# A layer's expert units on VectorE: two loops and one fixed buffer order

## The chip, the cores and the metric

The kernel runs on one core of one Trainium2 chip. The metric is device time in microseconds; the time before is the median of three runs.

## The reference

A trunk of two pre-norm residual layers over 256 tokens of width 2048. Layer 0 mixes tokens with a bidirectional mLSTM, layer 1 with grouped-query attention. After each mixer comes the same channel mixer, PEER, which is what the change touches:

```python
def peer(xn, wq, k1, k2, u, v):
    q = (xn @ wq).reshape(B, S, 8, 2, 128)
    s1, s2 = ...                      # scores of 8 heads against 128 + 128 keys
    t1, i1 = lax.top_k(s1, 16)
    t2, i2 = lax.top_k(s2, 16)
    cand_s = all 256 sums t1[a] + t2[b];  cand_i = i1[a] * 128 + i2[b]
    top_s, pos = lax.top_k(cand_s, 16)
    idx = cand_i at pos;  gate = softmax(top_s)
    # for each token and each of its 8 * 16 experts e, weight gate[e]:
    act = gelu(dot(x, u[idx]))
    y = sum over e of gate[e] * act[e] * v[idx]
```

Each token picks 16 experts per head out of 16384, and each expert is a row of u and a row of v, 2048 floats each.

## The kernel before

The work of a PEER layer is cut into 16 units: two blocks of 128 tokens by 8 heads. A unit has 16 tiles. A tile is one expert for each of the 128 tokens of the block: 128 rows of u and v together, 16 KB a row, 2 MB in all. So there are 256 tiles in a layer and 512 in the kernel.

Every tile goes the same way:

- POOL (`gathers`, the DMA at L551) waits on `v_used` until PE has used up the buffer and issues an indirect DMA from the table of experts into it. There are six buffers (`NUV = 6`, `uv_slot`), which lie in `ring_sb`. Tile t of a layer goes into buffer t mod 6 (`slot_of`), so a buffer's last tile is always the sixth before. POOL issues the gathers in order; once a unit it copies the 16 indices first (L539).
- VectorE (`expert`, L1683) waits for the landing of that buffer and takes the dot product of the u rows with the tokens, 128 x 2048. After each odd tile it handles two tiles together: `e_t` (L1690), `e_in` (L1692), `e_p` (L1694), and after ScalarE's tanh (L756) the weight `e_w` (L1696). In the last unit of a layer this is done for each tile alone.
- ScalarE (L760) writes the weight of each token into a diagonal 128 x 128 tile, `diag`.
- PE (L1211) multiplies `diag` by the v rows, adding up in four PSUM banks, and then counts up `v_used`, which frees the buffer.

Between its dots VectorE also chooses the experts of the next unit: `side_top`, `pair_top` and `chosen` stand behind the tiles `values_at`, `pairs_at` and `chosen_at` (5, 7 and 9 in the first eight units, 3, 5 and 7 in the others). In the first units of a layer PE also computes the router's queries (`router`) and scores for later heads, for which SyncE loads 2 MB a head (`load_queries`).

All this is written out: every engine's program has each unit's instructions once after the other. The only loops that turn more than once are those of SyncE over weight chunks (`load_chunks`, L442 to L444).

`Steps` (`did`, `need`) is how VectorE waits for its own results: `did` counts up a semaphore behind an instruction, `need` waits until it has reached a count. When layer 0 ends, SyncE loads the first weights of layer 1's mixer once PE has used all but two tiles: chunk 16 into `arena`, then the first two quarters of chunk 17 into `ring[10]` and `ring[11]`, which are buffer 5. The transposes of the next mixer's first rows and their norm (`norm_ms(2, 0)` in unit 9, POOL's power operation in unit 10, `norm_rows(2, 0, 3)` in unit 15) are fitted in among the last units.

Of the kernel before, what the change touches and what calls it, by code (L numbers as in the profile page):

```python
# [70 lines left out]
class Steps:  # L71
# [3 lines left out]
    def __init__(self, eng, sem):  # L75
        self.eng, self.sem, self.n, self.loop = eng, sem, 0, 0

    def did(self, ins):
        self.n += 1
        ins.then_inc(self.sem, 1)  # L80
        return self.loop + self.n

    def need(self, count):
        self.eng.wait_ge(self.sem, count)


def trunk_kernel(nc, consts, x, ln_mix, ln_ffn, m_w_in, m_gate_bias, m_head_norm, m_w_out,
# [21 lines left out]
    with ExitStack() as ctx:  # L109
# [176 lines left out]

        def slot_of(gu, k):

            return ((gu % UNITS) * TOPK + k) % NUV

        def uses(gu, k):

            earlier = sum(1 for t in range(LAYER_TILES) if t % NUV == slot_of(gu, k)) * (gu // UNITS)
            return earlier + ((gu % UNITS) * TOPK + k) // NUV + 1
# [138 lines left out]
        def _(sp):  # L433
# [71 lines left out]
        def _(pool):  # L505
# [27 lines left out]
            def gathers(l):  # L533

                quarters = 4 + 4 * (M_CHUNKS if l == 0 else ALL_CHUNKS)
                for u in range(UNITS):
# [36 lines left out]
        def _(act):  # L573
# [144 lines left out]
            def peer(l):  # L718
# [26 lines left out]
                def unit(u):  # L745
# [3 lines left out]
                    for k in range(TOPK):  # L749
# [8 lines left out]
                        for t in tiles:  # L758
                            act.wait_ge(v_used, gu * TOPK + (t + 1))
# [603 lines left out]
        def _(dve):  # L1363
# [16 lines left out]
            def side_top(l, su, heads_seen):  # L1380

                dve.wait_ge(sc_out, heads_seen)
                if su:
                    need(did(v.tensor_copy(scur[:, :], scores[:, su * (2 * P):(su + 1) * (2 * P)])))
# [44 lines left out]
            def chosen(gu):  # L1429

                dve.wait_ge(top_ready, gu + 1)
# [12 lines left out]
                if gu > 0:  # L1444
                    dve.wait_ge(idx_taken, gu)
                v.scalar_tensor_tensor(out=idx_next[:, :], in0=sel_if[:, 0:16], scalar=float(P),
                                       in1=sel_if[:, 16:32], op0=ALU.mult, op1=ALU.add).then_inc(idx_ready, 1)
                dve.wait_ge(gexp_ready, gu + 1)
# [222 lines left out]
            def peer(l):  # L1671
                def unit(u):
                    gu, b, more = l * UNITS + u, u // HEADS, u < UNITS - 1
                    need(st.n)
                    if gu:
                        dve.wait_ge(w_ready, gu * TOPK)
# [23 lines left out]
                    if u % HEADS == 0:  # L1700
                        dve.wait_ge(xn_ready, 2 * (2 * l + 1) + b + 1)
                    for k in range(TOPK):
                        expert(k)
                        if u == 2 and k == 12:
                            scale_block(l, 1)
                        if gu == HEADS + 1 and k == 0:
# [3 lines left out]
                        if gu == UNITS - 1 and k >= 12:  # L1710
                            dve.wait_ge(v_used, NUV + LAYER_TILES - 5)
                            lo_groups(dve, "n2", [k - 12])
                        if more and k == values_at:
                            head = min(u + 1, HEADS - 1)
                            pairs = side_top(l, u + 1, l * (HEADS + 1) + head + 2)
                        if more and k == pairs_at:
                            pair_top(gu + 1, pairs)
                        if more and k == chosen_at:
                            chosen(gu + 1)

                for u in range(UNITS):
                    unit(u)

# [212 lines left out]
```

## Time and profile before

| | |
|---|---|
| median of three runs | 3345.01 us (3344.4 to 3346.84) |
| profiled execution | 3349.07 us, its span 3346.9 us |
| busy share of the span | PE 86%, VectorE (DVE) 59%, ScalarE (ACT) 17%, GpSimd (POOL) 22% |
| HBM traffic | 1225.74 MB read, 367 GB/s over the span |
| gathers on queue q0 | 1073.77 MB, 75.8% of 16 engines' span |

The span is that of the profiled instructions; the time includes what lies around it. A busy PE is not PE at its peak, and idle time of an engine costs only where that engine, or what waits for it, sets the end. In a timeline the bracket behind a row is the idle time of the engine before it and what ended it.

### The profile page before, as it was taken

The numbers are of one execution on the slowest core, as the hardware profiler recorded it, in microseconds if no ns is written. First come the engines' busy times: TensorE is split into PE (matmuls) and PEld (weight loads), VectorE is DVE, ScalarE is ACT, GpSimd is POOL, SyncE is SP. The second block draws the span as 40 slices with busy tenths as digits, with TensorE's granted clock in tenths as the row PEclk, the third lists the DMA queues.
The fourth block names the chain that finished last, engine by engine and source line by source line (L and its number), as shares of the span: only waits on it lengthen the run. The fifth ranks groups of instructions, "written<-read, shape, count | busy, mean of one in ns | idle before, by whom it ended". The sixth has DMA issues, their size and how long they took to land.

```text
span 3346.9 us, 24916 instructions
## 1 busy us (share of the span) xinstructions
PE 2863.7 (86%) x8488; PEld 1572.2 (47%) x8488; DVE 1982.2 (59%) x3816; ACT 583.6 (17%) x1269; POOL 727.3 (22%) x571
## 2 busy tenths in 40 slices
PE   7999998888988777878879999888898787778777
PEld 6887864444443333333338786444454333333333
DVE  4454555555666666666665755555566666666665
ACT  4344311110111110010123531111111011000011
POOL 1000022322222222222210002222233222222221
PEclk9999999999998999899999999999999999999999
DMA  6544589999999999999985348999999999999998
GB/s 229 180 163 151 216 353 428 426 428 426 421 427 425 426 424 427 415 427 414 427 367 175 114 172 335 427 427 428 426 422 425 427 428 424 421 425 415 422 427 350
DMA packets 138749, 1229.45 MB, mean 367 GB/s; under 512 B 12928, under 2 KB 13696, under 8 KB 68096
## 3 DMA queue, kind: packets, MB, share of 16 engines
q0 software_dynamic: 73728, 1073.77, 75.8%
q1 hardware_dynamic: 61680, 147.99, 12.5%
q10 hardware_dynamic: 3216, 6.12, 0.5%
q8 instruction: 67, 1.10, 0.1%
q14 instruction: 58, 0.48, 0.0%
HBM read 1225.74 MB, written 2.10 MB: 367 GB/s over the span
## 4 chain that ended last, share of the span: by engine, by line
PE 49%; DMA 39%; DVE 7%; ACT 2%; issue 2%; POOL 0%; DVEq 0%; ACTq 0%; SPq 0%; POOLq 0%
DMA ring_sb<-in_peer_uv_dram,idx_cur 38%; PE bank L1211 25%; PE bank L936 15%; PE bank L983 5%; DVE ring_sb L1683 5%; ACT diag L760 1%; PE bank L995 1%; DVE w_parts L390 1%; ACT shared L756 0%; PE bank L1159 0%; ACT w_parts L384 0%; DMA ring_sb<-in_mlstm_w_out_dram 0%; DVE shared L1696 0%; PE bank L1018 0%; DVE shared L1692 0%
## 5 line engine op out<-in xcount | busy, mean ns | idle before, releaser
L1211 PE MATMUL bank<-ring_sb,diag 128*128 128x512 f32 x4096 | 1947.9, 631 | 439.6 <-ACT diag L760 439.6
L1683 DVE CUSTOM_DVE_ANT_0 ring_sb<-ring_sb,arena 128x2048 f32<-128x2048 f32 x512 | 1172.3, 2290 | 845.4 <-DMA ring_sb<-in_peer_uv_dram,idx_cur 845.4
L1211 PEld LDWEIGHTS bank<-ring_sb,diag 128*128 128x128 f32 x4096 | 805.5, 201 | 1540.6 <-issue 925.7
L551 POOL DMA_INDIRECT ring_sb<-in_peer_uv_dram,idx_cur x512 | 686.4, 1341 | 1872.1 <-PE bank L1211 1859.9
L936 PE MATMUL bank<-w_parts,actT_hi 128*128 128x512 f32 x1664 | 520.9, 394 | 9.3 <-DVE w_parts L390 7.7
L756 ACT ACTIVATE shared<-shared 128x2 f32<-128x2 f32 (+1 forms) x272 | 55.6, 205 | 2151.2 <-DVE shared L1692 2151.2
L390 DVE TENSOR_TENSOR w_parts<-ring_sb,w_parts 128x2048 fp32r<-128x2048 f32 x100 | 229.3, 2298 | 212.3 <-ACT w_parts L384 212.1
L936 PEld LDWEIGHTS bank<-w_parts,actT_hi 128*128 128x128 f32 x1664 | 310.2, 189 | 76.5 <-issue 12.5
L936 PE MATMUL bank<-w_parts,actT_lo 128*128 128x512 f32 x832 | 325.3, 391 | 0.0
L384 ACT CAST w_parts<-ring_sb 128x2048 fp32r<-128x2048 f32 x100 | 190.7, 1909 | 283.1 <-DMA ring_sb<-in_mlstm_w_in_dram 139.6
L760 ACT ACTIVATE diag<-const,shared 128x128 f32<-128x128 f32 x512 | 179.3, 394 | 90.1 <-DVE shared L1696 90.1
L936 PEld LDWEIGHTS bank<-w_parts,actT_lo 128*128 128x128 f32 x832 | 156.8, 188 | 33.3
L1696 DVE SCALAR_TENSOR_TENSOR shared<-shared 128x2 f32<-128x2 f32 (+1 forms) x272 | 44.1, 162 | 124.7 <-ACT shared L756 124.6
L983 PE MATMUL bank<-arena 128*128 128x256 f32 x512 | 114.7, 379 | 0.0
L983 PEld LDWEIGHTS bank<-arena 128*128 128x128 f32 x512 | 97.1, 190 | 23.4 <-issue 11.5
L983 PE MATMUL bank<-arena,wq_more 128*128 128x256 f32 x384 | 86.8, 379 | 0.0
L983 PEld LDWEIGHTS bank<-arena,wq_more 128*128 128x128 f32 x384 | 73.0, 190 | 20.2 <-issue 11.5
L526 POOL TENSOR_TENSOR small<-small,const 128x1 f32<-128x1 f32 x8 | 6.5, 818 | 275.7 <-DVE small L1470 222.7
L526 POOL TENSOR_TENSOR h_r<-h_ms,const 128x4 f32<-128x4 f32 x2 | 2.5, 1250 | 265.7 <-DVE h_ms L1627 265.7
L1692 DVE SCALAR_TENSOR_TENSOR shared<-shared 128x2 f32<-128x2 f32 (+1 forms) x272 | 44.0, 162 | 27.2 <-DVE shared L1690 0.9
L1690 DVE SCALAR_TENSOR_TENSOR shared<-shared 128x2 f32<-128x2 f32 (+1 forms) x272 | 44.0, 162 | 9.4
L526 POOL TENSOR_TENSOR q_r<-q_ms,const 128x8 f32<-128x8 f32 x5 | 12.5, 2505 | 139.0 <-DVE q_ms L1765 139.0
(169 smaller groups left out, 1090.7 us busy)
## 6 DMA issues: line engine op xcount, KB each, us to landing
ring_sb<-in_mlstm_w_in_dram SPq DMA_DIRECT2D x48, 1024.0 KB, 5.2
ring_sb<-in_attn_w_in_dram SPq DMA_DIRECT2D x20, 1024.0 KB, 5.2
ring_sb<-in_mlstm_w_out_dram SPq DMA_DIRECT2D x16, 1024.0 KB, 5.1
arena<-in_peer_wq_dram SPq DMA_DIRECT2D x16, 1024.0 KB, 11.4
ring_sb<-in_attn_w_out_dram SPq DMA_DIRECT2D x16, 1024.0 KB, 5.0
wq_more<-in_peer_wq_dram SPq DMA_DIRECT2D x12, 1024.0 KB, 15.8
ring_sb<-in_peer_uv_dram,idx_cur POOLq DMA_INDIRECT x512, 16.7
ring_sb<-in_peer_wq_dram SPq DMA_DIRECT2D x4, 1024.0 KB, 7.8
```

The source lines that it names most:

```text
L384: nc.scalar.copy(w_hi_of[j], w_raw(c, j)).then_inc(w_hi, 1)
L390: nc.vector.tensor_tensor(w_lo_of[j], w_raw(c, j), w_hi_of[j].bitcast(F32), ALU.subtract).then_inc(w_lo[j], 1)
L551: nc.gpsimd.indirect_dma_start(out=uv_slot[at], out_offset=None, in_=uv_rows, in_offset=bass.IndirectOffsetOnAxis(ap=idx_cur[par][:, k:k + ...
L756: nc.scalar.activation(e_th[:, c], e_in[:, c], ACT.Tanh, scale=GELU_C).then_inc(tanh_out, len(tiles))
L760: nc.scalar.activation(diag[slot_of(gu, t)][:, :], ident, ACT.Copy, scale=e_w[:, t:t + 1]).then_inc(diag_ready, 1)
L936: last = mm(acc[2 * par + b][:, :], xp, wp, start=(j == 0 and k == 0 and i == 0), stop=(j == 3 and k == QK - 1 and i == 2), skip_group_che ...
L983: last = mm(mis[0][:, side * T:(side + 1) * T], slots[half][:, k % 8, side * P:(side + 1) * P], yT[:, k, :], start=(k == 0), stop=(k == KT ...
L1211: last = mm(acc[n][:, :], diag[slot_of(gu, k)][:, :], v_slot[at][:, n * CH:(n + 1) * CH], start=False, stop=end and k == TOPK - 1, skip_gr ...
L1683: v.tensor_tensor_reduce(u_slot[at], u_slot[at], xn[b], 1.0, 0.0, ALU.mult, ALU.add, dots[:, k:k + 1]).then_inc(dot_done, 1)
L1690: need(did(v.scalar_tensor_tensor(out=e_t[:, c], in0=dots[:, c], scalar=GELU_A, in1=dots[:, c], op0=ALU.mult, op1=ALU.mult)))
L1692: v.scalar_tensor_tensor(out=e_in[:, c], in0=e_t[:, c], scalar=1.0, in1=dots[:, c], op0=ALU.add, op1=ALU.mult).then_inc(tanh_in, len(tiles))
L1696: v.scalar_tensor_tensor(out=e_w[:, c], in0=e_th[:, c], scalar=1.0, in1=e_p[:, c], op0=ALU.add, op1=ALU.mult).then_inc(w_ready, len(tiles))
```

## The change

VectorE's units 2 to 6 and 9 to 14 of each layer become the turns of two loops; units 0, 1, 7, 8 and 15 stay written out. For that every unit has to use the same buffers at the same places, so the tiles of a unit go into the six buffers in a fixed order of sixteen: 0, 1, 2, 3, 4, 5, 0, 1, 2, 3, 4, 0, 1, 2, 3, 5. POOL's and ScalarE's waits for a free buffer follow from it (`freed_at`). Inside a loop each wait's count is a register value that grows with the turn. The dot's own count (`dot_done`) is given up for `did` and `need`, and `e_p` now stands before `e_in`. What was to be done in a looped unit moves out: the scaling of the second token block to unit 1, the mean square for the next mixer to unit 15 and with it POOL's power operation. SyncE waits for the last tile before it loads into buffer 5.

```diff
     def need(self, count):
-        self.eng.wait_ge(self.sem, count)
+        self.eng.wait_ge(self.sem, count if self.turns is None else self.turns + count)
...
+        BUFFER_ORDER = (0, 1, 2, 3, 4, 5, 0, 1, 2, 3, 4, 0, 1, 2, 3, 5)
         def slot_of(gu, k):
-            return ((gu % UNITS) * TOPK + k) % NUV
+            return BUFFER_ORDER[k]
...
+        def freed_at(gu, k):
+            in_unit = [j for j in range(k) if BUFFER_ORDER[j] == BUFFER_ORDER[k]]
+            if in_unit:
+                return NUV + gu * TOPK + in_unit[-1] + 1
+            return NUV + (gu - 1) * TOPK + last_in_unit(BUFFER_ORDER[k]) + 1 if gu else 0
+
+        def last_used(l, slot):
+            return NUV + (l + 1) * LAYER_TILES - TOPK + last_in_unit(slot) + 1
...
                 if isinstance(c, int) and c == 16:
-                    act.wait_ge(v_used, NUV + LAYER_TILES - 3 + j)
+                    act.wait_ge(v_used, last_used(0, j))
...
                 sp.sem_inc(w_landed[j], 16)
+            sp.wait_ge(v_used, last_used(0, 5))
             for j in range(2):
                 load_quarter(a_w_in[0], slice(5 * CH, 6 * CH), w_raw(17, j), j)
...
-                        if l == 0 and u == HEADS + 2 and k == 2:
+                        if l == 0 and u == UNITS - 1 and k == 4:
                             norm(2, [0])
...
-                        pool.wait_ge(v_used, gu * TOPK + (k + 1))
+                        if freed_at(gu, k):
+                            pool.wait_ge(v_used, freed_at(gu, k))
...
-                        dve.wait_ge(uv_landed[at], 16 * uses(gu, k))
-                        v.tensor_tensor_reduce(u_slot[at], u_slot[at], xn[b], 1.0, 0.0, ALU.mult, ALU.add,
-                                               dots[:, k:k + 1]).then_inc(dot_done, 1)
+                        dve.wait_ge(uv_landed[at], later(16 * uses(gu, k), turn, 16 * BUFFER_ORDER.count(at)))
+                        n = did(v.tensor_tensor_reduce(u_slot[at], u_slot[at], xn[b], 1.0, 0.0, ALU.mult, ALU.add,
+                                                       dots[:, k:k + 1]))
...
-                        dve.wait_ge(dot_done, gu * TOPK + k + 1)
-                        need(did(v.scalar_tensor_tensor(out=e_t[:, c], in0=dots[:, c], scalar=GELU_A, in1=dots[:, c],
-                                                        op0=ALU.mult, op1=ALU.mult)))
+                        need(n)
+                        did(v.scalar_tensor_tensor(out=e_t[:, c], in0=dots[:, c], scalar=GELU_A, in1=dots[:, c],
+                                                   op0=ALU.mult, op1=ALU.mult))
+                        need(did(v.tensor_tensor(e_p[:, c], dots[:, c], gate_cur[:, c], ALU.mult)))
                         v.scalar_tensor_tensor(out=e_in[:, c], in0=e_t[:, c], scalar=1.0, in1=dots[:, c],
                                                op0=ALU.add, op1=ALU.mult).then_inc(tanh_in, len(tiles))
-                        need(did(v.tensor_tensor(e_p[:, c], dots[:, c], gate_cur[:, c], ALU.mult)))
-                        dve.wait_ge(tanh_out, gu * TOPK + k + 1)
+                        dve.wait_ge(tanh_out, later(gu * TOPK + k + 1, turn, TOPK))
...
-                        if u == 2 and k == 12:
+                        if u == 1 and k == 12:
                             scale_block(l, 1)
-                        if gu == HEADS + 1 and k == 0:
+                        if gu == UNITS - 1 and k == 0:
                             norm_ms(2, 0)
...
+                def units_in_loop(first, end):
+                    before = st.n
+                    with dve.Fori(0, end - first) as turn:
+                        st.turns = turn * UNIT_STEPS
+                        unit(first, turn)
...
-                for u in range(UNITS):
+                for u in (0, 1):
                     unit(u)
+                units_in_loop(2, HEADS - 1)
+                for u in (HEADS - 1, HEADS):
+                    unit(u)
+                units_in_loop(HEADS + 1, UNITS - 1)
+                unit(UNITS - 1)
```

The waits of `side_top`, `chosen` and the unit's head take `later(count, turn, step)` in the same way, which is `turn * step + count` inside a loop and `count` outside.

## Rows read from the trace of the kernel before

**Rows 1.** The page: busy time, granted clock and DMA share in 40 slices.
```profile
PE 2863.7 (86%) x8488; PEld 1572.2 (47%) x8488; DVE 1982.2 (59%) x3816; ACT 583.6 (17%) x1269; POOL 727.3 (22%) x571
...
PEclk9999999999998999899999999999999999999999
DMA  6544589999999999999985348999999999999998
```

**Rows 2.** The page: DMA queues, their packets, MB and share of 16 engines' span.
```profile
q0 software_dynamic: 73728, 1073.77, 75.8%
...
q8 instruction: 67, 1.10, 0.1%
q14 instruction: 58, 0.48, 0.0%
```

**Rows 3.** The page: costliest groups; count, busy us and mean ns, idle before and releaser.
```profile
L1211 PE MATMUL bank<-ring_sb,diag 128*128 128x512 f32 x4096 | 1947.9, 631 | 439.6 <-ACT diag L760 439.6
L1683 DVE CUSTOM_DVE_ANT_0 ring_sb<-ring_sb,arena 128x2048 f32<-128x2048 f32 x512 | 1172.3, 2290 | 845.4 <-DMA ring_sb<-in_peer_uv_dram,idx_cur 845.4
...
L551 POOL DMA_INDIRECT ring_sb<-in_peer_uv_dram,idx_cur x512 | 686.4, 1341 | 1872.1 <-PE bank L1211 1859.9
```

**Rows 4.** Timeline of VectorE: start, duration, instruction, idle before it.
```profile
873.55 2.29 DVE L1683 CUSTOM_DVE_ANT_0 ring_sb<-ring_sb,arena 128x2048 f32<-128x2048 f32 x1 [3.47 <-DMA ring_sb<-in_peer_uv_dram,idx_cur]
...
1399.14 2.29 DVE L1683 CUSTOM_DVE_ANT_0 ring_sb<-ring_sb,arena 128x2048 f32<-128x2048 f32 x1 [2.61 <-DMA ring_sb<-in_peer_uv_dram,idx_cur]
...
1401.82 0.15 DVE L1694 TENSOR_TENSOR shared<-shared 128x2 f32<-128x2 f32 x1
...
1404.04 2.29 DVE L1683 CUSTOM_DVE_ANT_0 ring_sb<-ring_sb,arena 128x2048 f32<-128x2048 f32 x1 [1.55 <-DMA ring_sb<-in_peer_uv_dram,idx_cur]
...
1409.90 2.29 DVE L1683 CUSTOM_DVE_ANT_0 ring_sb<-ring_sb,arena 128x2048 f32<-128x2048 f32 x1 [3.56 <-DMA ring_sb<-in_peer_uv_dram,idx_cur]
...
1422.90 0.16 DVE L1696 SCALAR_TENSOR_TENSOR shared<-shared 128x2 f32<-128x2 f32 x1 [0.36 <-ACT shared L756]
...
1429.52 2.29 DVE L1683 CUSTOM_DVE_ANT_0 ring_sb<-ring_sb,arena 128x2048 f32<-128x2048 f32 x1 [2.49 <-DMA ring_sb<-in_peer_uv_dram,idx_cur]
...
1489.32 2.29 DVE L1683 CUSTOM_DVE_ANT_0 ring_sb<-ring_sb,arena 128x2048 f32<-128x2048 f32 x1 [3.56 <-DMA ring_sb<-in_peer_uv_dram,idx_cur]
...
3257.59 2.29 DVE L1683 CUSTOM_DVE_ANT_0 ring_sb<-ring_sb,arena 128x2048 f32<-128x2048 f32 x1 [3.57 <-DMA ring_sb<-in_peer_uv_dram,idx_cur]
```

**Rows 5.** One unit's stretch: PE, PEld, DVE, ACT, POOL busy (count), clock, DMA, GB/s.
```profile
1411.00:1490.00 79.00, 61.45 (x128) 25.20 (x127) 48.92 (x103) 7.58 (x26) 19.81 (x17) 0.94 1.00 427
```

**Rows 6.** DMA queues in the stretch from 1406 to 1407 us.
```profile
q14 instruction: 1, 0.01, 2.0%
```

**Rows 7.** DMA queues in the stretch from 1427 to 1429 us.
```profile
q8 instruction: 1, 0.02, 3.4%
```

**Rows 8.** SyncE's register instructions in its loops: count, ns min/median/max.
```profile
L444 SPq ALU_OP  x69: 37/37/44, 29.8 to 1994.6; - x69
```

**Rows 9.** Timeline of VectorE: the dot of the odd tile after `side_top`.
```profile
1449.13 2.29 DVE L1683 CUSTOM_DVE_ANT_0 ring_sb<-ring_sb,arena 128x2048 f32<-128x2048 f32 x1 [0.87 <-DMA ring_sb<-in_peer_uv_dram,idx_cur]
```

**Rows 10.** Timeline of POOL: gathers, their start and duration.
```profile
1409.15 0.97 POOL L551 DMA_INDIRECT ring_sb<-in_peer_uv_dram,idx_cur  x1 [6.70 <-PE bank L1211]
...
1437.34 0.94 POOL L551 DMA_INDIRECT ring_sb<-in_peer_uv_dram,idx_cur  x1 [4.71 <-PE bank L1211]
1440.77 1.67 POOL L551 DMA_INDIRECT ring_sb<-in_peer_uv_dram,idx_cur  x1 [2.50 <-PE bank L1211]
...
2068.18 2.34 POOL L551 DMA_INDIRECT ring_sb<-in_peer_uv_dram,idx_cur  x1 [25.68 <-PE bank L1211]
```

**Rows 11.** Timeline of VectorE: the dot on what the last of these gathers brought.
```profile
2077.64 2.29 DVE L1683 CUSTOM_DVE_ANT_0 ring_sb<-ring_sb,arena 128x2048 f32<-128x2048 f32 x1 [0.92 <-DMA ring_sb<-in_peer_uv_dram,idx_cur]
```

**Rows 12.** Timeline of POOL and VectorE at the end of layer 0's unit 3.
```profile
775.44 0.94 POOL L551 DMA_INDIRECT ring_sb<-in_peer_uv_dram,idx_cur  x1 [4.20 <-PE bank L1211]
...
782.93 2.29 DVE L1683 CUSTOM_DVE_ANT_0 ring_sb<-ring_sb,arena 128x2048 f32<-128x2048 f32 x1 [1.38 <-DMA ring_sb<-in_peer_uv_dram,idx_cur]
```

More of the change, by code:

```diff
@@ L75, in __init__ @@
     def __init__(self, eng, sem):
-        self.eng, self.sem, self.n, self.loop = eng, sem, 0, 0
+        self.eng, self.sem, self.n, self.turns = eng, sem, 0, None
     def did(self, ins):
@@ L80, in did @@
         ins.then_inc(self.sem, 1)
-        return self.loop + self.n
+        return self.n
     def need(self, count):
-        self.eng.wait_ge(self.sem, count)
+        self.eng.wait_ge(self.sem, count if self.turns is None else self.turns + count)
 def trunk_kernel(nc, consts, x, ln_mix, ln_ffn, m_w_in, m_gate_bias, m_head_norm, m_w_out,
@@ L285, in trunk_kernel, with last_in_unit @@
         LAYER_TILES = UNITS * TOPK
+        BUFFER_ORDER = (0, 1, 2, 3, 4, 5, 0, 1, 2, 3, 4, 0, 1, 2, 3, 5)
+        assert len(BUFFER_ORDER) == TOPK and set(BUFFER_ORDER) == set(range(NUV))
         def slot_of(gu, k):
-            return ((gu % UNITS) * TOPK + k) % NUV
+            return BUFFER_ORDER[k]
+        def last_in_unit(slot):
+            return max(k for k in range(TOPK) if BUFFER_ORDER[k] == slot)
         def uses(gu, k):
-            earlier = sum(1 for t in range(LAYER_TILES) if t % NUV == slot_of(gu, k)) * (gu // UNITS)
-            return earlier + ((gu % UNITS) * TOPK + k) // NUV + 1
+            return gu * BUFFER_ORDER.count(slot_of(gu, k)) + BUFFER_ORDER[:k + 1].count(slot_of(gu, k))
+        def freed_at(gu, k):
[5 more added lines that the diff above has]
+            return NUV + (l + 1) * LAYER_TILES - TOPK + last_in_unit(slot) + 1
         FIRST_QUERY_SLOT = 5
@@ L758, in unit @@
                         for t in tiles:
-                            act.wait_ge(v_used, gu * TOPK + (t + 1))
+                            if freed_at(gu, t):
+                                act.wait_ge(v_used, freed_at(gu, t))
                             nc.scalar.activation(diag[slot_of(gu, t)][:, :], ident, ACT.Copy,
@@ L1378, in norm_rows, with later, side_top @@
                                        op0=ALU.mult, op1=ALU.mult).then_inc(xn_ready, 1)
-            def side_top(l, su, heads_seen):
-                dve.wait_ge(sc_out, heads_seen)
+            def later(count, turn, step):
+                return count if turn is None else turn * step + count
+            def side_top(l, su, heads_seen, turn=None):
+                if turn is None or su < HEADS:
+                    dve.wait_ge(sc_out, later(heads_seen, turn, 1))
                 if su:
-                    need(did(v.tensor_copy(scur[:, :], scores[:, su * (2 * P):(su + 1) * (2 * P)])))
+                    at = su * (2 * P)
+                    cols = slice(at, at + 2 * P) if turn is None else bass.ds(turn * (2 * P) + at, 2 * P)
+                    need(did(v.tensor_copy(scur[:, :], scores[:, cols])))
                 S = [scur[:, i * P:(i + 1) * P] for i in range(2)]
@@ L1427, in pair_top, with chosen @@
                 v.max(c_top[:, 8:16], crep[:, :]).then_inc(top_ready, 1)
-            def chosen(gu):
-                dve.wait_ge(top_ready, gu + 1)
+            UNIT_STEPS = 59
+            def chosen(gu, turn=None):
+                dve.wait_ge(top_ready, later(gu + 1, turn, 1))
                 settle(dve)
@@ L1444, in chosen @@
                 if gu > 0:
-                    dve.wait_ge(idx_taken, gu)
+                    dve.wait_ge(idx_taken, later(gu, turn, 1))
                 v.scalar_tensor_tensor(out=idx_next[:, :], in0=sel_if[:, 0:16], scalar=float(P),
                                        in1=sel_if[:, 16:32], op0=ALU.mult, op1=ALU.add).then_inc(idx_ready, 1)
-                dve.wait_ge(gexp_ready, gu + 1)
+                dve.wait_ge(gexp_ready, later(gu + 1, turn, 1))
                 need(did(v.reciprocal(g_rec[:, :], g_sum[:, :])))
@@ L1671, in peer, with unit @@
             def peer(l):
-                def unit(u):
+                def unit(u, turn=None):
                     gu, b, more = l * UNITS + u, u // HEADS, u < UNITS - 1
@@ L1675, in unit @@
                     if gu:
-                        dve.wait_ge(w_ready, gu * TOPK)
+                        dve.wait_ge(w_ready, later(gu * TOPK, turn, TOPK))
                     need(did(v.tensor_scalar(gate_cur[:, :], gate_next[:, :], 0.5, None, ALU.mult)))
@@ L1699, in unit @@
                     values_at, pairs_at, chosen_at = choice_at(u)
-                    if u % HEADS == 0:
+                    if u % HEADS == 0 and turn is None:
                         dve.wait_ge(xn_ready, 2 * (2 * l + 1) + b + 1)
@@ L1714, in unit @@
                             head = min(u + 1, HEADS - 1)
-                            pairs = side_top(l, u + 1, l * (HEADS + 1) + head + 2)
+                            pairs = side_top(l, u + 1, l * (HEADS + 1) + head + 2, turn)
                         if more and k == pairs_at:
@@ L1718, in unit @@
                         if more and k == chosen_at:
-                            chosen(gu + 1)
-                for u in range(UNITS):
-                    unit(u)
+                            chosen(gu + 1, turn)
+                def units_in_loop(first, end):
[3 more added lines that the diff above has]
+                        unit(first, turn)
+                    st.turns = None
+                    assert st.n - before == UNIT_STEPS, st.n - before
+                    st.n = before + UNIT_STEPS * (end - first)
+                for u in (0, 1):
+                    unit(u)
+                units_in_loop(2, HEADS - 1)
[3 more added lines that the diff above has]
+                unit(UNITS - 1)
             peer(0)
```

2 lines of the change are left out of this document (1 added, 1 removed).

## The prediction

> **What bounds the kernel now.** [...] One unit's stretch shows 427 GB/s and PE busy 61 of 79 us [rows 5]. So the experts' gathers set the pace: 512 of them, 2 MB each, 75.8% of the span on their queue alone [rows 2, 3]. The groups say the same from the other side: the dots on VectorE (L1683) idle 845 us for a landing, and POOL's gathers (L551) idle 1860 us for PE to free a buffer [rows 3]. POOL waits so long because it issues early. What counts is whether the transfers run dry.
>
> They don't, and they beat time: dots that wait for a landing start 4.9 us apart (1399.14, 1404.04) [rows 4], about 4.905 us over many. Once a unit one is late: 1409.90 is 5.86 us after 1404.04. The idle time before the late dot is 3.56 us where its neighbours have 1.5 to 2.6. It comes back at 1489.32. From 873 to 3258 us I count 24 such steps, each 0.96 to 0.98 us; the first and the last stand in the rows [rows 4]. In the stretch of the step at 1409.90, from 1406 to 1407 us, the queues show one packet of kind instruction on q14 [rows 6]; the same holds at each of the steps that I opened. Whose is it? PE has 16976 matmuls and weight loads [rows 1] and 67 fetches of 1.10 MB in all on q8, so a fetch is 16.4 KB or about 253 instructions, 65 bytes each; q14's 58 fetches are 8.3 KB, so about 128 instructions [rows 2]. VectorE counts 103 instructions in a unit [rows 5], and the waits that stand alone come on top, some 130 together: one block a unit, as the steps show. ScalarE and POOL have under half of that, and q14 packets lie between the steps too, with no late dot behind them. PE's fetches leave no step either [rows 7]. I read this so: one DMA engine carries VectorE's fetches, is a tile behind the others, and each landing waits for it. Each of VectorE's fetches then costs the beat 0.97 us. A unit is 16 x 4.905 + 0.97 = 79.4 us, which is the distance of the late dots at 1409.90 and 1489.32 us.
>
> **The change, part by part.** *Loops.* Of the 16 units of a layer 5 and 6 become turns of two loops. The code that VectorE runs through once falls by 4 + 5 = 9 units a layer, 18 in all. If the body stays in VectorE's instruction store, 18 fetches go: 18 x 0.97 = 17.5 us gained. The body is longer than a unit now: each count that depends on the turn has to be computed into a register before its wait. From the code that is 16 landings, 24 waits around dots, products and tanh, three at the unit's head and some 20 in the choice of experts, so about 64 more, near 200 instructions, 1.5 blocks. Four bodies x 70 / 128 = 2.2 blocks more, 2.1 us given back.
>
> Those computing instructions take 37 ns on SyncE [rows 8]; I put one at 75 ns with its issue. Most lie in front of a landing that VectorE waits for anyway. The tightest place is the choice: after its first part comes the dot of an even tile, and then VectorE idles 0.87 us for the next landing [rows 9]. Nine of them there are 0.7 us, just covered. If that cover were gone, the surplus (0.1 to 0.5 us) would only shorten the ring's reserve below. At the unit's end VectorE is done at 1423.06, and the second dot of the next unit starts at 1429.52 [rows 4]; less one dot of 2.29 us and 0.2 us of small work that leaves 4 us for a branch and what it fetches. So a stall of that size costs nothing by itself.
>
> *Product before e_in.* L1694 (0.15 us) now stands before L1692 and has to end before it. The chain of a pair of tiles grows by 0.1 to 0.2 us, 272 times. It lies behind transfers already in flight: nothing, except from the reserve.
>
> *The fixed order.* A buffer was refilled six tiles after its use, always. Now the tiles at 0 to 3 and 11 to 14 of a unit follow the fifth before them, 5 to 10 the sixth, 4 and 15 the tenth. POOL issues in order, so 4 and 15 only follow their neighbours. What does a distance of five leave? From an odd landing (1429.52) to the gather into its even partner's buffer 7.8 us pass (1437.34), to that of its own 11.25 us (1440.77) [rows 10]. Where the clock was at its lower level in between it is 1.7 us more, as 1399.14 to 1409.15 shows. A gather into an idle queue takes 9.5 us from issue to its dot (2068.18 to 2077.64, with a POOL instruction of 2.34 us instead of 0.94), so 8.1 to 9.5 [rows 10, 11]. Distance five gives 24.5 us from landing to landing. For an even tile 24.5 - 4.9 - 7.8 - 8.1 = 3.7 us stay over, for an odd one 5.1; with the low clock 2.0 and 3.4. No dry spell there. In the first units of a layer PE also does the router's queries. There the gather at 775.44 follows tile 11; now the tile that landed at 782.93 would follow it. 775.44 + 8.1 = 783.5, so 0.6 us late [rows 12]. Some 4 to 5 such units a layer at 0.6 to 1.1 us, where clock or POOL add to it: I take 5 us in all. The bounds are 0 and, for 12 units at 1.1 us, 13 us.
>
> *What moves.* SyncE now waits for the last tile before it loads the first half of chunk 17. ScalarE may split it only when PE has used the same quarter of chunk 16, which PE begins after the last tile and leaves after half of its 96 matmuls; the 1 MB of a quarter take 2.5 us at 427 GB/s: nothing. Behind that wait stand only later weights. The square mean and POOL's small power operation move to unit 15 and sit in POOL's queue before a gather whose buffer was freed ten tiles ago: nothing. If POOL were late there, the gathers behind it would have the 3.7 us. Scaling the second block one unit earlier finds VectorE idle in every beat.
>
> Sum: -17.5 + 2.1 + 5 = -10.4 us. The profiled execution took 3349.07 us, 2.2 us of it outside its span, so 3338.7 us; it stood 4.1 us above the median of the three runs, which makes 3334.6, said as **3335 us**.
>
> The trace has no loop on VectorE, so whether the body stays is not shown. SyncE's loops, 23 turns with four loads each, are far shorter than a block and say nothing about 200 instructions. The bound on one side is no fetch per return, on the other three or four.
>
> [...]
>
> **Rivals.** *The body is fetched again on every return (slower).* A body of 200 covers two or three blocks; if the store holds the current and the next block only, the way forward drops the first. A return then fetches two or three blocks where a unit now has one: 18 x 1 to 2 x 0.97 = 17.5 to 35 us, with the 7 us of order and longer code 25 to 42 us: 3370 to 3387, I say 3380. Three more per return would be 3404. It decides as soon as a return fetches more than one block. For it: each crossing fetches exactly one block, in step, which is how a small store would look. Against it: a store that holds four such blocks would look the same.
>
> *Another DMA engine takes the slow one's place.* Without VectorE's fetches the slowest is whoever PE's 16.4 KB fetch hits, once a unit. If these all fall on one engine they cost as much as the steps that went: 18 x 0.97 is not gained, 3345 to 3352, at most a hair faster. Against it: these fetches left no step in any beat [rows 7].
>
> *The ring of five starves.* With register work, low clock and slow POOL instructions together the reserve of 2.0 us could be used up in every unit; 32 x 0.5 to 0.8 us would be 16 to 25 us, less the 15 us of fetches: 3346 to 3355. It decides once the pair's chain grows by over 2 us.
>
> **How the numbers follow.** The forecast (3328 to 3340) has 0.50, the repeated fetch 0.32, the other engine 0.10, the starved ring 0.08. What the measurement can tell from no change is 0.2%, 6.7 us. The forecast's upper end and the second rival give most of "same". Faster 0.47, same 0.17, slower 0.36. The range has to reach into the repeated fetch; 3324 to 3385 leaves out its worst third and little else. For the forecast alone it is 3326 to 3341.
>
> **What would show it.** Right: q14 with about 40 packets instead of 58; in units 3 to 6 and 10 to 14 no late dot, 16 beats in 78.5 us; in the first units of a layer the dot of a unit's first tile up to 1 us late. Wrong: q14 with 75 or more packets and two or three steps of 0.97 us in each looped unit; or steps that stay and stand beside q8 packets; or idle slices of DMA in the looped units.

## The result, and the profile after

The changed kernel takes 3369.89 us (median of six runs, 3366.09 to 3371.52), the kernel before beside it 3345.57 us (3344.4 to 3348.69). The ratio is 1.0069, 95% interval 1.0056 to 1.0082: 24 us slower, where 10 us faster was forecast. The profiled execution's span is 3367.1 us, 20.2 us above that of before.

The page of the changed kernel, with the lines that answer to [rows 1 to 3]:

```profile
PE 2874.8 (85%) x8488; PEld 1576.2 (47%) x8488; DVE 1984.5 (59%) x3816; ACT 583.2 (17%) x1269; POOL 694.0 (21%) x571
...
PEclk9999999999999899989999999999999999999999
DMA  6554689999999999999995358999999999999998
GB/s 232 175 168 145 233 343 410 407 409 402 415 413 427 413 419 428 427 421 427 427 409 173 121 169 336 422 418 414 411 406 406 426 428 424 418 426 427 426 427 374
...
q0 software_dynamic: 73728, 1073.77, 75.8%
...
q8 instruction: 67, 1.10, 0.1%
q14 instruction: 41, 0.34, 0.0%
...
L1231 PE MATMUL bank<-ring_sb,diag 128*128 128x512 f32 x4096 | 1959.8, 634 | 450.3 <-ACT diag L780 450.1
L1713 DVE CUSTOM_DVE_ANT_0 ring_sb<-ring_sb,arena 128x2048 f32<-128x2048 f32 x512 | 1172.4, 2290 | 846.3 <-DMA ring_sb<-in_peer_uv_dram,idx_cur 846.2
L570 POOL DMA_INDIRECT ring_sb<-in_peer_uv_dram,idx_cur x512 | 644.4, 1259 | 1930.9 <-PE bank L1231 1900.0
```

Busy times hardly move, and the DMA digits of the slices stay at nine. What shows the loss is the line of GB/s: in the first slices of each layer's expert units it stands at 402 to 422, later at 413 to 428. And q14 has 41 packets instead of 58: VectorE fetches less, as the change meant.

So I cut the units where the slices change. The next two fences hold the windows from the dot of tile 15 of unit 0 to that of unit 5, the units with router work; columns as in [rows 5]. First the kernel before, layer 0 and layer 1:

```profile
525.58:942.21 416.63, 366.01 (x1002) 190.00 (x1001) 248.09 (x511) 44.26 (x145) 117.20 (x86) 0.95 1.01 426
...
2123.17:2539.30 416.13, 367.84 (x999) 190.40 (x998) 248.01 (x512) 44.03 (x145) 116.99 (x85) 0.96 1.01 426
```

Then the changed kernel, the same two stretches, the rest of layer 0's units, and one looped unit:

```profile
528.61:958.93 430.32, 369.66 (x998) 190.62 (x997) 248.49 (x512) 43.91 (x145) 110.08 (x85) 0.94 0.99 410
...
2135.48:2563.99 428.51, 374.63 (x1004) 193.30 (x1003) 248.50 (x512) 43.91 (x145) 106.71 (x85) 0.94 0.99 411
...
958.93:1752.74 793.81, 631.35 (x1334) 262.30 (x1333) 495.16 (x1020) 85.21 (x279) 205.74 (x169) 0.94 1.00 423
...
1358.34:1436.80 78.46, 60.31 (x122) 24.63 (x121) 49.47 (x103) 7.59 (x26) 19.30 (x16) 0.91 1.01 427
```

Units 1 to 5 are 13.7 and 12.4 us longer, 26.1 together, and their rate falls from 426 to 410 GB/s; the rest of the kernel wins 6 us back. The last row is what the forecast promised for a looped unit: 16 beats in 78.5 us instead of 79.4. It is one of the best. From first dot to first dot, the twelve looped units 9 to 14 of both layers take 78.4 to 80.4 us, 79.05 in the mean, where the kernel before has 79.5; five of them are at 78.4 to 78.6. So the loops give something, though not in every unit. Something else eats more than they give, and it sits where TensorE computes router queries.

One late refill, seen from three sides. VectorE in the changed kernel, the dots of layer 0's unit 2, tiles 12 to 14 (start, duration, idle before):

```profile
688.36 2.29 DVE L1713 CUSTOM_DVE_ANT_0 ring_sb<-ring_sb,arena 128x2048 f32<-128x2048 f32 x1 [3.23 <-DMA ring_sb<-in_peer_uv_dram,idx_cur]
693.53 2.29 DVE L1713 CUSTOM_DVE_ANT_0 ring_sb<-ring_sb,arena 128x2048 f32<-128x2048 f32 x1 [2.87 <-DMA ring_sb<-in_peer_uv_dram,idx_cur]
701.11 2.29 DVE L1713 CUSTOM_DVE_ANT_0 ring_sb<-ring_sb,arena 128x2048 f32<-128x2048 f32 x1 [4.18 <-DMA ring_sb<-in_peer_uv_dram,idx_cur]
```

POOL's gathers there, of which the second brings tile 14:

```profile
681.79 3.04 POOL L570 DMA_INDIRECT ring_sb<-in_peer_uv_dram,idx_cur  x1 [2.50 <-PE bank L1231]
688.68 2.78 POOL L570 DMA_INDIRECT ring_sb<-in_peer_uv_dram,idx_cur  x1 [3.85 <-PE bank L1231]
691.76 0.93 POOL L570 DMA_INDIRECT ring_sb<-in_peer_uv_dram,idx_cur  x1 [0.30 <-issue]
```

And the window in which nothing was left to transfer (the last two columns are the DMA engines' busy share and GB/s):

```profile
691.00:693.50 2.50, 2.50 (x11) 1.81 (x11) 0.00 (x0) 0.00 (x0) 1.60 (x3) 1.00 0.63 203
```

Read them together. Until 688.68 us TensorE had not freed the buffer. The gather then took 2.78 us instead of 0.94, and another 9.65 us went by until its dot, 12.4 us in all; meanwhile the engines ran dry, 203 GB/s, and tile 14 came 7.58 us after tile 13 instead of 4.9. In units 1 to 5 of both layers I count 22 such refills (dot over 5.2 us after the one before, gather ended less than 4.2 us before that earlier dot), the first at 537.2 us, the last at 2553.7, at tiles 12 to 14 and 0, two at 2 and 3. Together they are 27.7 us above the beat, near the 26.1 us that these units lose. The two need not be equal: the loops also save fetches in these units, and part of a delay is caught up behind it.

The same count in the other kernels' traces is the clearest sign. The kernel before has none, and so have e2, e3, e6, e7, e8, e9 and e11 below. The order without loops (e1) has 18, e12 has 18, e10 five, e4 three and e5 one. The granted clock has hardly a part in it: in the 20 us before the earlier dot it was 1.0 for 17 of the 22 refills and 0.91 to 0.93 for the others.

TensorE in the changed kernel, from tile 7 of unit 1 on, shows why buffers are late (a row without a bracket had no idle time before it):

```profile
582.80 3.62 PE L1003 MATMUL bank<-arena 128*128 128x256 f32 x16
586.26 7.03 PE L1231 MATMUL bank<-ring_sb,diag 128*128 128x512 f32 x16
593.12 3.62 PE L1003 MATMUL bank<-arena 128*128 128x256 f32 x16
...
617.22 10.46 PE L1231 MATMUL bank<-ring_sb,diag 128*128 128x512 f32 x24
634.72 5.48 PE L1231 MATMUL bank<-ring_sb,diag 128*128 128x512 f32 x8 [7.04 <-ACT diag L780]
```

A part of a router query and two tiles take 10.32 us; two landings take 9.81. From the end of tile 7 to the unit's end, 582.8 to 627.7 us, TensorE works without a pause and falls back, so it frees late what the tiles behind tile 7 used. In the kernel before it works just so, without a pause from 579.1 to 627.5 us with the same 10.32 us for two tiles, and no refill is late. A distance of six tiles had room for that, one of five has not.

### The profile page after: what moved, and what is told of

It is laid out like the page before. It is cut to its first block, busy times and chain, and to the rows that moved or that the text cites. A ratio compares the mean times of both kernels' runs of the same rounds, so it can differ in the third digit from the quotient of the medians.

```text
span 3367.1 us, 26013 instructions
## 1 busy us (share of the span) xinstructions
PE 2874.8 (85%) x8488; PEld 1576.2 (47%) x8488; DVE 1984.5 (59%) x3816; ACT 583.2 (17%) x1269; POOL 694.0 (21%) x571
## 3 DMA queue, kind: packets, MB, share of 16 engines
q1 hardware_dynamic: 61680, 147.99, 12.4%
## 4 chain that ended last, share of the span: by engine, by line
PE 48%; DMA 38%; issue 6%; DVE 4%; ACT 2%; POOL 1%; SPq 0%; DVEq 0%; ACTq 0%; POOLq 0%
DMA ring_sb<-in_peer_uv_dram,idx_cur 37%; PE bank L1231 24%; PE bank L956 15%; PE bank L1003 5%; DVE ring_sb L1713 2%; ACT diag L780 1%; POOL ring_sb L570 1%; PE bank L1015 1%; ACT shared L775 1%; ACT w_parts L401 0%; DMA x_sb<-in_x_dram 0%; DVE shared L1726 0%; DVE shared L1723 0%; PE bank L1179 0%; PE bank L1038 0%
## 5 line engine op out<-in xcount | busy, mean ns | idle before, releaser
L570 POOL DMA_INDIRECT ring_sb<-in_peer_uv_dram,idx_cur x512 | 644.4, 1259 | 1930.9 <-PE bank L1231 1900.0
L1713 DVE DVE_READ_ACCUMULATOR2_ANT shared<- 128x1 f32 x512 | 42.3, 83 | 0.0
```

The costliest lines, as they stand in the source:

```text
L570: nc.gpsimd.indirect_dma_start(out=uv_slot[at], out_offset=None, in_=uv_rows, in_offset=bass.IndirectOffsetOnAxis(ap=idx_cur[par][:, k:k + ...
L1713: n = did(v.tensor_tensor_reduce(u_slot[at], u_slot[at], xn[b], 1.0, 0.0, ALU.mult, ALU.add, dots[:, k:k + 1]))
```

## The experiments

Each ratio is to the kernel before, measured beside it on the same chip; 0.1% is 3.3 us. The last two columns are the profiled units 1 to 5 of layer 0 and layer 1, between the same dots as above (before 416.6 and 416.1).

| kernel | median us | ratio, 95% interval | q14 packets | units 1-5 |
|---|---|---|---|---|
| changed | 3369.89 | 1.0069 (1.0056-1.0082) | 41 | 430.3, 428.5 |
| e1 order alone | 3377.69 | 1.0100 (1.0085-1.0116) | 59 | 426.7, 428.1 |
| e2 old order | 3345.72 | 0.9994 (0.9985-1.0003) | 58 | 415.6, 416.4 |
| e3 late loop only | 3339.51 | 0.9981 (0.9972-0.9990) | 49 | 415.7, 415.2 |
| e4 order shifted | 3339.14 | 0.9978 (0.9969-0.9988) | 42 | 418.3, 415.6 |
| e5 with TensorE loop | 3335.66 | 0.9966 (0.9952-0.9979) | 42 | 417.8, 415.7 |
| e6 changed, less router | 3330.80 | 0.9949 (0.9936-0.9963) | 41 | 415.6, 415.2 |
| e7 body of three | 3357.68 | 1.0030 (1.0018-1.0042) | 67 | 416.3, 415.3 |
| e8 body of two | 3352.50 | 1.0012 (1.0002-1.0021) | 62 | 415.1, 416.0 |
| e9 late loops, both engines | 3339.26 | 0.9977 (0.9968-0.9986) | 50 | 416.3, 415.3 |
| e10 shifted, no loop | 3351.48 | 1.0009 (1.0000-1.0018) | 58 | 420.5, 417.6 |
| e11 before, less router | 3344.78 | 0.9993 (0.9985-1.0002) | 58 | 417.0, 416.4 |
| e12 router earlier | 3362.89 | 1.0037 (1.0022-1.0053) | 41 | 422.0, 423.3 |

**Order or loops.** The changed kernel with every unit written out:

```diff
-                units_in_loop(2, HEADS - 1)
...
-                units_in_loop(HEADS + 1, UNITS - 1)
...
+                for u in range(0, UNITS):
+                    unit(u)
```

> The changed kernel with all sixteen units of a layer written out: fixed order, product before e_in and the moves stay, no loop. Theory A (the order costs: where PE computes router queries, the refill of a buffer that was used five tiles ago is issued too late): +25 to +45 us on the kernel before, that is 3370 to 3390, with the loss in units 0 to 5 of each layer, and q14 back at 58 to 60 packets. Theory B (the loops cost: register instructions and branches delay VectorE, the order alone costs the 5 us of the prediction): 3345 to 3355.

The order alone is slower than the changed kernel, and q14 is back at 59. In its profiled execution units 1 to 5 are 10.1 and 12.0 us longer, with no loop in the code; that execution, 3371.76 us, was the fastest of its four (up to 3383.18), so the trace shows less than the median's loss. Theory A holds, B falls. The control keeps everything but the order, a row of buffers for each unit now, always the sixth tile before:

```diff
-        BUFFER_ORDER = (0, 1, 2, 3, 4, 5, 0, 1, 2, 3, 4, 0, 1, 2, 3, 5)
+        ORDER = ("0123450123450123",
+                 "4501234501234501",
+                 "2345012345012345",
...
```

> As the first, and the order of buffers is the old one again (always the sixth tile before). What is left of the change is the product before e_in, did and need for the dot, and what moved. Theories A and B both: no change, 3340 to 3351. If it is slower by 10 us or more, the small edits cost it and both theories are wrong.

No change: the product before e_in, `did` and `need` around the dot, and all that moved cost nothing. The order costs 1.0100 - 0.9994 = 1.06%, 35 us; by the medians, 32. By the two intervals it is some 6 us more or less.

**Where the short distances stand.** With a row for each unit, only the looped units need equal ones. First with a loop only where there is no router work: units 0 to 8 in the old order, 9 to 14 with the first row below, 15 with the second:

```diff
+                 "0123450123401235",
...
+                 "4012350123450123")
...
-                units_in_loop(2, HEADS - 1)
```

> Units 0 to 8 of each layer written out in the old order, units 9 to 14 in a loop with the fixed order, unit 15 written out. Theory A: the reserve of the ring is enough without router work, 10 to 12 fetches go at 0.97 us each, about 1 us comes back for the longer body: 3333 to 3338. Theory B: the six looped units cost as much as in the changed kernel: 3345 to 3358. Theory C (PE's fetches take the place of VectorE's as the step of the slowest DMA engine): 3342 to 3348.

Then both loops, with the order turned so that the eight refills after five tiles stand at tiles 3 to 6 and 8 to 11. The first row is that of units 2 to 6, the second of 8 to 14; units 0, 1, 7 and 15 have the old order:

```diff
+                 "2340123501234501",
...
+                 "0124501345012345",
```

> Both loops as in the changed kernel, another fixed order: the refills that follow the fifth tile stand at tiles 3 to 6 and 8 to 11 of a unit instead of 0 to 3 and 11 to 14, and the units that are written out (0, 1, 7, 15) have the old order. Theory A: the late refills were those of tiles 11 to 3, right behind the router's work; most of the loss goes, 3328 to 3342. Theory B: the loops cost, whatever the order: 3360 to 3372. Theory C: 3340 to 3348.

Both beat the kernel before. With the same loops, and as many short distances in each looped unit, the place (and the old order in four written-out units) is worth 1.0069 - 0.9978 = 0.91%, 30 us. Units 1 to 5 are back at 418.3 and 415.6 us. The kernel e3 came 1.5 us above its range: 0.13% under the control, 4.4 us (6.2 by the medians), for some 9 fetches (58 to 49), a half to seven tenths of their price of 8.7. And is the turned order free? The kernel e4 with all units written out:

> The shifted order with all units of VectorE written out. It isolates the place of the short distances. Theory A, all of it: the shifted order leaves enough reserve, 3343 to 3349 us, units at 79.4 us again. If the shifted order still costs something in the router units: 3350 to 3358 us, and the loops then gained 11 to 19 us in the kernel that had both.

Perhaps not quite. It is 0.15% above the control, 5 us, and its time lies in the second case's range; but the two intervals overlap. The trace is on that side: units 1 to 5 are 4.9 and 1.2 us longer than in e2 and hold the five late refills. Between e10 and e4 the loops give 0.31%, 10.4 us, less than the 11 to 19 expected; between e1 and the changed kernel also 0.31%.

**The router.** Changed kernel and kernel before, each with a quarter of the router's matmuls:

```diff
-                    for k in range(8 * half, 8 * half + 8):
+                    for k in (8 * half, 8 * half + 7):
```

> The changed kernel (3369.9 us), with 2 of the 8 matmuls in each part of a router query; the queries and so the choice of experts are other ones, the number of gathers is the same. Theory A (TensorE frees the buffers late because of the router's work, and five buffers in turn have no reserve for it): most of the loss goes, 3338 to 3350. Rival: the query weights that are loaded in these units, or the loops, make the loss: 3362 to 3372.

> The kernel before, with 2 of the 8 matmuls in each part of a router query, as in the changed kernel's run of that kind (ratio 0.9949). If the router's work costs the old order nothing, 3342 to 3349 us: then the fixed order's whole price lies in the router's work, and without it the loops give some 15 us. If the kernel before gains 8 us or more, part of that run's gain is the router's own.

The window of units 1 to 5 of layer 0 in e6:

```profile
525.57:941.19 415.62, 327.75 (x761) 145.82 (x760) 248.96 (x512) 43.91 (x145) 91.95 (x85) 0.93 1.00 424
```

TensorE is busy 327.8 us instead of 369.7, and the stretch falls from 430.3 to 415.6 us. The same edit gives the kernel before nothing (0.9993). The time, 3330.80 us, is 7 us under the range expected: not most of the loss went, but all of it, and the loops' gain came out. So what the order costs needs the router's work beside it, and the query weights, still loaded in full, do not cost it by themselves. Both kernels of this kind compute other queries, so they choose other experts, as many. Without that work the loops and the order together give 0.9993 - 0.9949 = 0.44%, 14.7 us (by the intervals some 5 us more or less); the prediction had 15.4 for the loops.

The same from the other side, with all work kept and only its place changed:

```diff
-            return {7 + 2 * i: (u + 2, i) for i in range(4)} if u + 2 < HEADS else {}
+            return {3 + 2 * i: (u + 2, i) for i in range(4)} if u + 2 < HEADS else {}
```

> The changed kernel with the four parts of a router query behind tiles 3, 5, 7 and 9 of a unit instead of 7, 9, 11 and 13, all work kept. The refills of tiles 0 to 3, which follow 11 to 14, then come after TensorE has caught up; those of tiles 11 to 14, which follow 6 to 9, stay late. Theory A: about half of the loss goes, 3348 to 3362 us. If the place of the router's work beside the short distances does not matter: 3366 to 3373 us.

It is 0.32% (11 us) faster than the changed kernel, just short of the range. Runs of it spread from 3349.6 to 3371.4, and the profiled one, 3370.98, is among the slowest, so its trace shows no gain in all. Units 1 to 5 win back 8.3 + 5.2 = 13.5 of the 26.1 us, half as expected, but unit 0 of the two layers lasts 92.6 and 90.6 us from its first dot to its last instead of 86.6 and 83.8, which takes the same back. So this run supports the place only weakly; e4 is the stronger one. The new cost in unit 0 was not followed up.

**TensorE's fetches.** In e4, units 9 to 14 of TensorE as a loop too:

```diff
+                        pe.wait_ge(diag_ready, count if turn is None else turn * TOPK + count)
...
-                for u in range(HEADS, UNITS):
-                    unit(u)
+                for u in (HEADS,):
+                    unit(u)
+                with pe.Fori(0, UNITS - HEADS - 2) as turn:
+                    unit(HEADS + 1, turn)
+                unit(UNITS - 1)
```

> As the kernel with the shifted order (3339.1 us), and TensorE's units 9 to 14 of each layer are a loop as well. Theory C (once VectorE's fetches are gone, TensorE's 16 KB fetches are the steps that remain in units 9 to 14): q8 falls from 67 to 55 to 60 packets, the steps of 1.4 to 2 us in units 9 to 14 go, 3331 to 3336 us. Rival: those steps have another cause: q8 falls, the time stays at 3337 to 3341. Second rival: a body of about 260 TensorE instructions does not stay: q8 at 75 or more, 3342 to 3352.

> The kernel with the late loop only (old order in units 0 to 8, ratio 0.9981), and TensorE's units 9 to 14 a loop too. If the first loop gains nothing, because late refills in the router units cost what its saved fetches give, this one is as fast as the shifted order with TensorE's loop (ratio 0.9966 to the kernel before): 3333 to 3338 us, with q14 at 49 and q8 at 57 packets. If the first loop is worth its 4 to 8 us, 3339 to 3343 us.

The packets on q8 fall from 67 to 57 in both, so TensorE's body stays. The two queues move apart: with TensorE's loop q14 has 42 packets in e4 and in e5, 49 in e3 and 50 in e9, and with VectorE's loops alone q8 stays at 67 while q14 falls from 58 to 41. So the packets of q8 are TensorE's fetches, and those that went from q14 are VectorE's. How many instructions one of q8 brings can be estimated from e6 and e11: 672 matmuls and 672 weight loads fewer than before (7816 of each for 8488), and 61 packets for 67, so 1344 / 6 = 224 a packet, 192 to 269 with one packet more or less; the prediction's 253 lies in that. The step itself can be seen in e3 (VectorE's dots; then the queues from 3011 to 3012 us):

```profile
3003.43 2.29 DVE L1729 CUSTOM_DVE_ANT_0 ring_sb<-ring_sb,arena 128x2048 f32<-128x2048 f32 x1 [2.60 <-DMA ring_sb<-in_peer_uv_dram,idx_cur]
3008.34 2.29 DVE L1729 CUSTOM_DVE_ANT_0 ring_sb<-ring_sb,arena 128x2048 f32<-128x2048 f32 x1 [1.50 <-DMA ring_sb<-in_peer_uv_dram,idx_cur]
3014.48 2.29 DVE L1729 CUSTOM_DVE_ANT_0 ring_sb<-ring_sb,arena 128x2048 f32<-128x2048 f32 x1 [3.84 <-DMA ring_sb<-in_peer_uv_dram,idx_cur]
```

```profile
q8 instruction: 1, 0.02, 6.9%
```

4.91 us, then 6.14: a step of 1.2 us beside a q8 packet, in a unit where VectorE fetches nothing. Three of the twelve q8 packets in e3's units 9 to 14 have such a step, 1.2 to 1.5 us; the others show none over 0.6 us, and why was not followed up. In e9, with TensorE's loop, layer 1's units 9 to 14 have none; layer 0's unit 12 still has one of 1.2 us, beside a q8 packet at 1427.8 us. But what it is worth stays open: e5 against e4 is 0.12% and e9 against e3 0.04%, and the intervals overlap in both pairs. The fastest full kernel of all is e5, 0.34% (11 us) faster than the kernel before. Whether the first loop pays at all (e5 against e9, which has none) is not settled either: their intervals overlap too, and e9's 3339.26 us lies at the lower end of the range for a first loop that pays.

**How long may a body be?** Loops of two and three units in place of one, in units 9 to 14 of each layer:

```diff
-                    with dve.Fori(0, end - first) as turn:
-                        st.turns = turn * UNIT_STEPS
-                        unit(first, turn)
+                    with dve.Fori(0, (end - first) // BODY) as turn:
+                        st.turns = turn * (UNIT_STEPS * BODY)
+                        for i in range(BODY):
+                            unit(first + i, turn)
```

> As the kernel with the late loop only (3339.5 us, q14 49 packets), with a body of two units, about 400 instructions, and three turns. If it stays: q14 at 49 to 52 packets, 3338 to 3342 us. If it is fetched again on each of the two returns: q14 at 59 to 68 packets, 3344 to 3354 us.

> Old order of buffers everywhere, and units 9 to 14 of each layer in a loop of two turns with three units each, a body of about 600 VectorE instructions (48 tiles are a multiple of six, so each turn has the same buffers). If such a body stays in VectorE's store: q14 at 51 to 54 packets, 3339 to 3344 us. If it is fetched again on the second turn: q14 at 60 to 68 packets, 3344 to 3352 us.

A body of three units is fetched again: q14 at 67, 0.30% slower than before although the order is the old one, and 5.7 us above the range expected. The body of two units does both. VectorE's fetches in e8 in units 10 to 15, in layer 0 from 1262 to 1738 us, then in layer 1 from 2860 to 3335 us:

```profile
q14 instruction: 5, 0.04, 0.0%
...
q14 instruction: 16, 0.13, 0.1%
```

The same loop, once kept and once fetched on every turn. The two copies differ in where they begin in the program and so perhaps in how many fetched blocks they touch; that this decides is a guess that no run tested.

What a missed return costs stands in VectorE's first instruction of unit 11, the first after a return, in e8, layer 0 and layer 1:

```profile
1348.71 0.25 DVE L1725 TENSOR_SCALAR shared<-shared 128x16 f32<-128x16 f32 x1 [0.48 <-DVE shared L1744]
...
2948.85 0.17 DVE L1725 TENSOR_SCALAR shared<-shared 128x16 f32<-128x16 f32 x1 [5.84 <-issue]
```

In layer 0 VectorE goes on after 0.48 us; in layer 1 it stands for 5.84 us and waits for nothing that the profile shows. So it is at all four returns that fetch (two in e8's layer 1, one a layer in e7): 5.6 to 6.2 us. The loops there take 4.0 to 5.4 us longer per such return: units 9 to 14 of layer 1 take 486.1 us in e8 and 475.5 in e3, and in e7 481.0 and 481.9 in the two layers against 477.0 and 476.5 in e2. With that fits that e7 is 0.36% (12 us) above the control e2, where nine packets more at 0.97 us would make 8.7.

## Why the prediction was wrong, point by point

**The step that failed** is "The fixed order": "I take 5 us in all. The bounds are 0 and, for 12 units at 1.1 us, 13 us." It measured 35 us (e1 against e2). Its place was right, the router units, and so was the doubt about POOL; the clock had hardly a part in it (1.0 before 17 of the 22). Three parts of the working were wrong:

- *The time from a gather to its dot.* The prediction took 8.1 to 9.5 us from a gather into an idle queue [rows 10, 11]. The 22 late ones took 8.2 to 13.2 us. For 20 of them it was over 9.5. 16 are POOL instructions of 2 us or longer; that of 688.68 us starts 0.32 us after a dot's start (688.36, 2.29 us long) and ends 0.8 us after the dot's end, while the one behind it, 691.76, beside no dot, takes 0.93. The whole trace says the same. Of the changed kernel's 512 gathers 180 start while a dot runs, and 177 of them end 0.8 to 1.0 us after that dot's end; of the 332 others 326 take under 1 us. The kernel before has the same pattern (223 start while a dot runs, 220 of them end 0.8 to 1.0 us after its end, and 285 of the 289 others take under 1 us), so this is no new cost: a late refill only has no reserve to hide it in.
- *How many tiles are late.* One gap, at tile 0 of a unit, was opened [rows 12] and priced once a unit. But TensorE is behind from tile 7 on, and of the eight tiles that the refills after five tiles follow, 6 to 9 and 11 to 14, seven lie there. 22 late refills in ten units are two a unit, at 1.3 us each (27.7 / 22), where 0.6 to 1.1 was taken.
- *What a late landing does next.* Reserve was worked out from gapless landings. TensorE stays busy at 10.32 us for two tiles, so a tile that lands late doesn't let it catch up in between; the next short distance can find it as late as before. This is argued from the rows of TensorE, no run took it apart.

One reading beside it was off as well and decided nothing. The way from 1399.14 to 1409.15 us is 10.0 us, at a granted clock of 0.83 where the way from 1429.52 to 1437.34 had 1.00, so an even tile has 2.2 us less at the low clock, not 1.7, and 1.5 us stay over, not 2.0.

**Loops:** "If the body stays in VectorE's instruction store, 18 fetches go: 17.5 us gained", less 2.1 for longer bodies. The body stayed and q14 fell by 17. Five of the twelve looped units 9 to 14 take the 78.5 us that was named; the mean is 79.05, with steps beside q8 packets in two of them. Worth: 14.7 us where the order costs nothing (e11 to e6), 10.4 us beside late refills (e10 to e4, e1 to changed). Right in mechanism and nearly in size; that a step costs less beside late refills fits, but the intervals of the two worths overlap.

**Repeated fetch,** the likelier of the slower rivals at 0.32, gave 3380 us and came close to the time for a reason that isn't there: 41 packets, not 75. The range, 3324 to 3385 us, holds the measured time only because it reached into this rival; that is luck. The trace decides here, not the number. Its price was wrong too: it took 0.97 us for each block more, and a return that fetched cost 4.0 to 5.4 us (for longer bodies, e7 and e8), because VectorE stands still meanwhile; the 4 us that were to cover a branch and its fetch are less than those 5.6 to 6.2 us. It was no idle fear, though: e7 shows it at three units and e8 at two, in one layer. By the prediction's 200 a unit, an estimate, the bodies of one, two and three units are 200, 400 and 600 instructions: the first stayed, the second did in one layer of two, the third did not.

**Another DMA engine takes the slow one's place:** in part. PE's fetches left no step in the rows of before; in e3, where VectorE's fetches are gone, 1.2 us steps stand beside q8. They come in a few units, not 18. That one engine carries VectorE's fetches is the prediction's reading; no row names a DMA engine, but the trace bears it out. A gather's landing comes in 16 parts, the semaphore counts that the dot waits for, and each has its time. In the kernel before, each of the 24 steps between 873 and 3258 us has a q14 packet 2.0 to 4.5 us before the landing. The last of the 16 parts falls behind the fifteenth by another 0.96 to 1.12 us there, and the fifteenth keeps its beat, 4.75 to 4.91 us. At 1409.88 us the last part is 5.41 us behind, at the landing before it 4.44. The q8 packet at 1427.38 us moves the fifteenth part by 0.98 us instead, from 5.41 to 4.43 us ahead of the last, and the last comes on its beat of 4.90 us: this fetch was covered. In e3 the last part stands 0.09 us behind the fifteenth at 3008.31 us, and 1.24 us at 3014.45, after the q8 packet at 3011.25: nothing was left to cover it.

**The ring starves** had 0.08 and 3346 to 3355 us, with a pair's chain that grows, in every unit. A ring that starves is what happened, but from TensorE's side and in the router units alone.

**Product before e_in, the moves, the branch, register work:** nothing, as said. For the first two e2 shows it, for the last two the looped units that take 78.5 us, 16 beats and no more.

## What to carry to other kernels

A ring's reserve has to be read where its slowest consumer is most behind, not in the average unit: take for each refill the time at which its buffer would be free under the new distance, and ask how long a transfer needs there. If a loop forces an uneven order, put the short distances where that engine has caught up; eight short distances a unit cost 35 us at one place and some 5, near the noise, at another. And count fetch packets before and after making a loop: the body that stayed saved 17 fetches at 18 returns, and a body of three units that was fetched again cost 12 us more than the same code without a loop (e7 against e2), because the engine stood still at each return, 5.6 to 6.2 us.

## What the runs showed of the hardware

- One VectorE body was kept in one layer (5 fetches in 476 us) and fetched again each turn in the other (16 in 475 us), from the same source lines; why the two differ is open. A return that fetched stopped VectorE for 5.6 to 6.2 us (four of four); in the returns that did not, it stood for 0.4 to 0.5 us.
- In the kernel before, the last of a gather's 16 parts falls another 0.96 to 1.12 us behind the fifteenth beside 24 q14 packets, and the dot is as late; where it was 5.41 us behind, a q8 packet that moved another part by 0.98 us delayed no dot.
- Landings are late by 1.2 to 1.5 us beside three of twelve fetches of TensorE (16 KB) in e3's looped units, where most of VectorE's 8 KB fetches (0.97 us in the kernel before) are gone.
- A POOL gather that starts while a dot of VectorE runs ends 0.8 to 1.0 us after the dot's end (177 of 180 in the changed kernel, where the longest took 3.3 us); 326 of the 332 others take under 1 us.
